# Inverses of the delta-rule blocks in a two-layer hybrid backbone: 8 by 8 diagonal blocks by forward substitution on GpSimd, the highest level in quarters of 64

## What is computed

```python
decay = _masked_exp(gam[..., :, None] - gam[..., None, :], incl)
a_strict = jnp.where(strict, jnp.einsum('bchtk,bchsk->bchts', kb, kc) * decay, 0.0)
lhs = a_strict + jnp.eye(CHUNK, dtype=a_strict.dtype)
sol = lax.linalg.triangular_solve(lhs, rhs, left_side=True, lower=True, unit_diagonal=True)
```

## Time and profile before

| what | value |
|---|---|
| runs listed | 2750.91, 2751.10, 2753.89 us, median 2751.1 |
| profiled execution: span | 2753.8 us (the slowest listed time is 2753.89) |
| TensorE busy | 2452.9 us, 89% |
| VectorE busy | 1261.2 us, 46% |
| ScalarE busy | 653.6 us, 24% |
| GpSimd busy | 609.6 us, 22% |
| scans of layer 0 | about 307 to 657 us |
| scans of layer 1 | about 1752 to 2043 us |

### The profile page before, as it was taken

The page is one execution under the profiler, slowest core; times in us unless marked ns, Lnnn a source line. Parts: engine busy times, 40 slices in busy tenths (PEclk is TensorE's granted clock), DMA queues, the critical chain, the costliest instruction groups (busy, mean ns, idle before and its releaser), DMA issues.

```text
span 2753.8 us, 45775 instructions
## 1 busy us (share of the span) xinstructions
PE 2452.9 (89%) x15116; PEld 1641.3 (60%) x15117; DVE 1261.2 (46%) x2828; ACT 653.6 (24%) x1191; POOL 609.6 (22%) x640
## 2 busy tenths in 40 slices
PE   5999888888989999999996898888888999999996
PEld 2437788887745555555554345788876555555553
DVE  4442487877433333333333453467863333333333
ACT  2116342432201111111111214523221111111111
POOL 0000244532002222222221000235320122222221
PEclk9999899999989999999998899999999999999997
DMA  7642200002539999999996352200026899999994
GB/s 264 244 168 80 32 1 1 1 1 67 229 111 349 358 357 350 337 343 340 363 339 194 133 184 61 50 1 1 1 67 263 305 370 369 387 353 367 372 367 158
DMA packets 187953, 574.27 MB, mean 209 GB/s; under 512 B 55774, under 2 KB 99110, under 8 KB 148902
## 3 DMA queue, kind: packets, MB, share of 16 engines
q1 hardware_dynamic: 162982, 520.48, 50.8%
q0 software_dynamic: 24832, 51.97, 8.0%
HBM read 554.89 MB, written 53.15 MB: 221 GB/s over the span
## 4 chain that ended last, share of the span: by engine, by line
PE 62%; DMA 13%; DVE 12%; issue 5%; ACT 4%; POOLq 2%; DVEq 2%; ACTq 1%; POOL 0%; SPq 0%
PE ps L1815 56%; DMA featT<-ffn_rows,idx_in 8%; PE ps L1819 5%; DVE R L1157 3%; DMA R<-ffn_rows,idx_in 3%; ACT R L864 2%; POOLq L776 1%; DMA R<-in_exp_up 1%; DVE R L1436 1%; DVE ring L1157 1%; DVE featT L1157 1%; DVE R L1160 1%; DVEq L1154 1%; ACT L864 1%; DVE h L1157 1%
## 5 line engine op out<-in xcount | busy, mean ns | idle before, releaser
L1815 PE MATMUL ps<-R 128*64 128x256 f32 (+6 forms) x9232 | 1433.8, 379 | 62.9 <-DVEq L1441 16.0
L1815 PEld LDWEIGHTS ps<-R 128*64 128x64 f32 (+2 forms) x9232 | 887.2, 162 | 476.2 <-issue 251.7
L864 ACT ACTIVATE R<-ps 128x256 f32<-128x256 f32 (+3 forms) x395 | 175.4, 444 | 1073.0 <-PE ps L1815 1027.4
L1157 DVE TENSOR_TENSOR R<-R,ps 128x256 f32<-128x256 f32 (+2 forms) x256 | 151.0, 590 | 445.9 <-ACT R L864 367.1
L1815 PE MATMUL ps<-featT,ring 128*128 128x512 f32 (+1 forms) x768 | 312.8, 564 | 0.3 <-issue 0.3
L1815 PEld LDWEIGHTS ps<-featT,ring 128*128 128x128 f32 x768 | 147.0, 195 | 161.4 <-issue 156.5
L1160 DVE TENSOR_SCALAR R<-ps,idx_out 128x512 f32<-128x512 f32 x128 | 96.1, 751 | 271.4 <-PE ps L1815 271.4
L1815 PE MATMUL ps<-ring,R 128*128 128x128 f32 (+2 forms) x1008 | 205.9, 331 | 15.4 <-DVE ring L1157 9.5
L1166 DVE COPY R<-ps 128x512 f32<-128x512 f32 (+2 forms) x280 | 153.8, 549 | 131.4 <-PE ps L1819 101.7
L701 POOL TENSOR_TENSOR R<-ring,lev 128x512 f32<-128x512 f32 x56 | 72.2, 1290 | 614.1 <-DVEq L1398 308.4
L800 POOL DMA_INDIRECT ffn_sum_even<-R,idx_out x64 | 94.5, 1476 | 482.1 <-DVE idx_in L1157 354.9
(11 more groups left out here) (200 smaller groups left out, 1989.3 us busy)
## 6 DMA issues: line engine op xcount, KB each, us to landing
R<-in_exp_gate SPq DMA_DIRECT2D x128, 1024.0 KB, 9.4
R<-in_exp_up SPq DMA_DIRECT2D x128, 1024.0 KB, 19.2
R<-in_exp_down SPq DMA_DIRECT2D x128, 1024.0 KB, 19.3
R<-in_w_mod SPq DMA_DIRECT2D x48, 1024.0 KB, 6.9
ring<-in_w_in SPq DMA_DIRECT2D x30, 1024.0 KB, 5.3
ring<-in_w_out SPq DMA_DIRECT2D x4, 1024.0 KB, 6.8
R<-in_w_out SPq DMA_DIRECT2D x4, 1024.0 KB, 6.4
ffn_sum_odd<-zero SPq DMA_DIRECT2D x6, 512.0 KB, 11.1
```

The source lines that it names most:

```text
L864: do(C.activation(out_, in_, func, **kw), name)
L1157: do(V.tensor_tensor(out_, a, b, op), name)
L1815: return MM(out_, lhsT, rhs, start=start, stop=stop)
```

## The change

The three lowest levels go. In their place, for each unit, the 8 by 8 blocks on the diagonal are inverted by substitution:

1. ScalarE copies the four 32x32 diagonal squares of each head out of A (`own_quarters`, four copies of 32 rows).
2. GpSimd masks and folds them to one 8-column block per row, and spreads each element against the unit vectors (`own_blocks`, four operations).
3. TensorE multiplies by a block-of-ones matrix, so that every row of an 8-block holds all elements of its block (`repeats`, one product of 256 columns); ScalarE copies that out (`repeats_copy`).
4. GpSimd does seven dependent steps of a multiplication and a subtraction of 4 to 28 elements per row, and writes the result with one 128x512 product as block diagonal into W (`own_inverse`).
5. TensorE transposes the four heads, ScalarE copies them to the other half of W.

Three levels follow as before (`MID` = 3, blocks of 16, 32, 64), with both halves of W of one layout. The highest level works on quarters: 4 products of 64x64, a copy of 64 rows, 4 products of 64x64, and a negated copy by ScalarE straight into W. The work that stood between seven levels is dealt out again over these steps; `levels_abs` and `levels_exp` now stand together at the end of a unit on ScalarE (`states`), `keys(u + 1)` stands before the third subtraction on VectorE, and VectorE has no subtraction of a highest level. Seven operations are added to VectorE's constants at the start. Waits on `sp_x`, `sp_done` and `cum_dve` become waits on one counter, `sp_dve`.

```diff
+BLK = 8
+L0 = 3
+MID = LEVELS - 1 - L0
+NP, NQ = 2 * MID + 3, 2 * MID + 1
...
+                def own_blocks(u):
+                    wait("dq_sb", u + 1, l)
+                    do(G.tensor_tensor(dq[:, :, :], dq[:, :, :], blkq[:, :].unsqueeze(1).to_broadcast([P, HH, 32]), ALU.mult))
+                    do(G.tensor_tensor(d16[:, :, :], dq[:, :, 0:16], dq[:, :, 16:32], ALU.add))
+                    do(G.tensor_tensor(dc[:, :, :], d16[:, :, 0:BLK], d16[:, :, BLK:16], ALU.add))
+                    if u:
+                        wait("pre_ps", 3 * u, l)
+                    do(G.tensor_tensor(dx[:, :, :], dc[:, :, :].rearrange("p q t -> p (q t)").unsqueeze(2).to_broadcast([P, HH * BLK, BLK]),
+                                       unit8[:, :].unsqueeze(1).to_broadcast([P, HH * BLK, BLK]), ALU.mult), "nt_ready")
+                def own_inverse(u):
+                    d = UNITS[u][1]
+                    do(G.tensor_copy(dv[:, :, :], unit8[:, :].unsqueeze(1).to_broadcast([P, HH, BLK])))
+                    wait("rep_sb", u + 1, l)
+                    rep = dr[:, :, :].rearrange("p (q t) r -> p q t r", q=HH)
+                    for n in range(BLK - 1):
+                        r, to = (n, slice(n + 1, BLK)) if d == 0 else (BLK - 1 - n, slice(0, BLK - 1 - n))
+                        do(G.tensor_tensor(dt8[:, :, to], rep[:, :, to, r], dv[:, :, r:r + 1].to_broadcast([P, HH, BLK - 1 - n]), ALU.mult))
+                        do(G.tensor_tensor(dv[:, :, to], dv[:, :, to], dt8[:, :, to], ALU.subtract))
+                    if u >= 2:
+                        wait("vn_ps", u - 1, l)
+                    do(G.tensor_tensor(W[u % 2][:, 1, :, :].rearrange("p q (b t) -> p q b t", t=BLK), dv[:, :, :].unsqueeze(2).to_broadcast([P, HH, P // BLK, BLK]),
+                                       blk[:, :].rearrange("p (b t) -> p b t", t=BLK).unsqueeze(1).to_broadcast([P, HH, P // BLK, BLK]), ALU.mult), "nt_ready")
...
+                own_blocks(0)
+                own_inverse(0)
                 masked(0, 0)
...
-                    masked(u, 2)
                     if wanted:
                         do(levels_mul(late, u, hq[:, :, tk(c)]), "hl_ready")
-                    masked(u, 3)
+                    masked(u, 2)
-                    masked(u, 4)
-                    masked(u, 5)
-                    masked(u, 6)
...
+                        own_blocks(u + 1)
+                        own_inverse(u + 1)
                         masked(u + 1, 0)
                         masked(u + 1, 1)
...
+                def own_quarters(u):
+                    wait("at_ready", 2 * u + 1, l)
+                    if u:
+                        wait("nt_ready", (u - 1) * (MID + 2) + 1, l)
+                    for b in range(4):
+                        own = slice(32 * b, 32 * b + 32)
+                        ins = C.activation(dq[own, :, :], AT[u % 2][own, :, own], ACT.Identity)
+                    do(ins, "dq_sb")
+                def repeats_copy(u):
+                    wait("pre_ps", 3 * u + 3, l)
+                    f(dr[:, :, :].rearrange("p a r -> p (a r)"), ps[:, 1, 2 * P:4 * P], ACT.Identity, "rep_sb")
...
+                def states(u):
+                    levels_abs(u)
+                    levels_exp(u)
...
-                levels_abs(0)
                 e_gdn(0)
+                own_quarters(0)
+                repeats_copy(0)
+                states(0)
...
-                    levels_exp(u)
+                    for hf in range(2):
+                        half_copy(u * NP + hf + 1, hf, W[u % 2][:, 0, :, :])
                     if un > 1:
                         wait("ho_ps", un - 1, l)
                     f(eb[:, :], bh[:, :], ACT.Exp, "eb_ready")
-                    if u + 1 < U:
-                        steps(Mg, u + 1, range(HS, NDEC))
-                    act.drain().then_inc(S["m_ready"], 1)
-                    for j in range(1, LEVELS):
...
+                    wait("p_ps", (u + 1) * NP, l)
+                    f(Pm[hi, :, 0:HD], ps[hi, 1, 0:HH * HD].rearrange("p (h t) -> p h t", h=HH), ACT.Identity, "p_sb")
+                    if u + 1 < U:
+                        own_quarters(u + 1)
+                    wait("q_ps", (u + 1) * NQ, l)
+                    f(W[u % 2][lo, 1, :, hi], ps[lo, 3, 0:HH * HD].rearrange("p (h t) -> p h t", h=HH), ACT.Identity, "p_sb", scale=-1.0)
+                    if u + 1 < U:
+                        repeats_copy(u + 1)
...
                     if u + 1 < U:
-                        levels_abs(u + 1)
+                        states(u + 1)
...
+            ts(levt[:, 1, :], levt[:, 0, :], L0, None, ALU.logical_shift_right)
+            cp(blk[:, :], levt[:, 1, :])
+            ts(blk[:, :], blk[:, :], 0.0, None, ALU.is_equal)
+            tt(blkq[:, :], blk[:, 0:32], blk[:, 32:64], ALU.add)
+            for b in range(2, 4):
+                tt(blkq[:, :], blkq[:, :], blk[:, 32 * b:32 * b + 32], ALU.add)
+            do(V.tensor_reduce(unit8[:, :], ident[:, :].rearrange("p (b r) -> p r b", r=BLK), AX.X, ALU.add))
...
-                    w_first(u)
                     if u:
                         hgrn_out(u - 1)
+                    if u:
                         hgrn_state(u - 1)
                         scores(u - 1)
-                    w_next(u, 1)
-                    if u:
-                        gdn_end(u - 1)
...
-                    w_next(u, 2)
+                    w_next(u, 0)
                     if u:
+                        gdn_end(u - 1)
                         ssd_out(u - 1)
+                    w_next(u, 1)
                     if wanted:
                         h_levels(u, 0)
-                    w_next(u, 3)
                     if u:
                         ssd_state(u - 1)
                     if more_:
                         hgrn_scans(u + 1)
+                        keys(u + 1)
+                    w_next(u, 2)
                     if wanted:
                         h_levels(u, 1)
                     if more_:
+                        queries(u + 1)
                         hgrn_levels(u + 1, (0, 1))
-                    w_next(u, 4)
-                    if more_:
-                        keys(u + 1)
-                        queries(u + 1)
                     if wanted:
                         h_levels(u, 2)
                     if more_:
                         hgrn_levels(u + 1, (2, 3))
-                    w_next(u, 5)
                     if wanted:
                         h_levels(u, 3)
                     if more_:
                         hgrn_levels(u + 1, (4, 5, 6))
-                    w_next(u, 6)
...
+                def repeats(u):
+                    wait("nt_ready", u * (MID + 2) + 1, l)
+                    mm(ps[:, 1, 2 * P:4 * P], blk[:, :], dx[:, :, :].rearrange("p a r -> p (a r)")).then_inc(S["pre_ps"], 1)
+                repeats(0)
...
+                    wait("nt_ready", u * (MID + 2) + 2, l)
+                    for hf in range(2):
+                        for q in range(2):
+                            ins = turn(ps[:, 1 + hf, tk(q)], Wu[:, 1, 2 * hf + q, :])
+                        ins.then_inc(S["p_ps"], 1)
...
+                        for hf in range(2):
+                            wait("p_sb", u * (NP + 1) + 2 * a + hf + 3, l)
+                            for q in range(2):
+                                got, tq = Pm[:, 2 * hf + q, :], Wu[:, 1, 2 * hf + q, :]
+                                mm(ps[:, (3, 0)[hf], tk(q)], tq, got)
+                                ins = mm(ps[:, (3, 0)[hf], tk(2 + q)], got, tq)
+                            ins.then_inc(S["q_ps"], 1)
...
+                    wait("t_ready", 2 * (u + 1) * MID, l)
+                    for q in range(HH):
+                        ins = mm(ps[hi, 1, q * HD:(q + 1) * HD], AT[u % 2][lo, q, hi], Wu[lo, 0, q, lo])
+                    ins.then_inc(S["p_ps"], 1)
+                    if wanted:
+                        wait("h_cp", (un - 1) * 4 + 2, l)
+                        h_products(u, 2)
+                    wait("p_sb", (u + 1) * (NP + 1) - 1, l)
+                    for q in range(HH):
+                        ins = mm(ps[lo, 3, q * HD:(q + 1) * HD], Pm[hi, q, 0:HD], Wu[hi, 1, q, hi])
+                    ins.then_inc(S["q_ps"], 1)
+                    if more_:
+                        repeats(u + 1)
+                    if wanted:
+                        wait("h_cp", (un - 1) * 4 + 3, l)
+                        h_products(u, 3)
+                        wait("m_ready", 3 + 2 * u, l)
+                        wait("at_ready", 2 * u + 4, l) if more_ else wait("ssd_sb", 2 * u, l)
+                        decays(u, Ms, HS, 6).then_inc(S["ssd_pre"], 1)
+                    if not last_step:
...
+                    h_out(u)
```

220 lines of the change are left out of this document (104 added, 116 removed).

## The result

| | runs shown | median | ratio to before (95% interval) |
|---|---|---|---|
| before | 2748.89 to 2757.23 us (5) | 2751.1 us | |
| changed | 2762.22 to 2778.12 us (5) | 2769.5 us | 1.0061 [1.0046, 1.0076] |

The account below looks back on a forecast made before the run. Outputting units were taken as bound by VectorE and TensorE taking turns, context units by the levels' latency. Startup +1.9, layer 0 -35.6 and layer 1 +5.5 gave -28.2 from 2751.1: 2723 us, range 2690 to 2765.

Parts of the forecast that it names:

- the period becomes 36: Scan units giving output: time from one unit's finished inverse to the next falls from 42 us to 36.
- the clock rival: TensorE idles longer per unit, so its clock falls; outputting intervals about 4 us longer, 2754 us in all; chance 0.14.
- the same 8: Layer 0's six full intervals: 8 us of low clock kept from before, added to 6 x 36 for 224.
- my own walk: Step-by-step timing of one outputting unit across the engines, from one inverse's end to the next: 36 us.
- Price of the small GpSimd operation: Each of fourteen dependent substitution operations on GpSimd: 0.44 us with its gap, in all 6.2 us.
- The chain rival: Slower GpSimd substitution steps lengthen every unit; the gain is gone at 0.62 us an operation; chance 0.18.
- ScalarE and not GpSimd releases the first level: Outputting units: ScalarE's copies after the levels' Abs and Exp start the first level, with 1.1 us to spare for GpSimd.
- VectorE alone sets the period, 33: Rival for outputting units: TensorE and VectorE overlap better, intervals of 33 us, total 2696 us; chance 0.18.
- Context interval 32.2: Layer 1's units without output: the uncovered chain gives 30.2 us, plus 2.0 for low clock, 32.2.
- Last interval 31.6: Last unit of a layer's scan, which prepares no next one: from 34.3 to 31.6 us, -2.7.
- Tail 18.1: From a layer's last finished inverse to the next stage: 18.1 us, +8.8 in each layer.
- First units: First scan unit of each layer: -7 us in layer 0, +3.5 in layer 1.

Follow-up runs that it names:

- the runs with fillers: The changed kernel with TensorE products nothing reads, placed where it idles; with 13 per unit at the unit's head alone: 2726.0 us, ratio 0.9896.
- with 10 fillers: The changed kernel with 5 unread TensorE products ahead of the replicating product and 5 ahead of the block transposes: 2731.0 us, ratio 0.992.
- The other order of ScalarE alone: The changed kernel with ScalarE's exponentials of the levels behind the two copies of the transposed blocks, not ahead: 2746.1 us, ratio 0.997.
- the run with three steps: The changed kernel with 3 of the 7 GpSimd substitution steps, its inverse not the right one: 2760.9 us, ratio 1.0022.
- kernels with head fillers: Changed kernels with unread TensorE products ahead of the replicating product and the block transposes; with 5 and 8: 2726.0 us, ratio 0.9896.

## Why the prediction was wrong

**The step that failed** is "the period becomes 36", with the sentence under the clock rival that "outputting units keep TensorE at work through most of the chain". From forecast to profile the span is 50.8 us longer (2776.4 against 2753.8 - 28.2). The eight outputting intervals that follow an outputting unit make 49.8 of it: six in layer 0 took 266.0 for 224 and two in layer 1 83.2 for 75.4; the other terms, each off by up to 6 us, cancel to 1.0. The mechanism was named as a rival at a chance of 0.14, and at half its size: it priced +4 an interval from one row at 0.89, but the clock fell three times per interval to a mean of 0.81, +8.3. In the sum, the term for the low clock was "the same 8" for six intervals; it measured 266.0 - 216 = 50. The rival, too, forecast no change where it was slower. The Trainium skill's rule of the clock gate was cited as speaking against the change, and it was right about the direction; the runs with fillers are what shows it.

Why it was mis-sized can be read in my own walk. It had TensorE waiting for the spread, for the copies and for VectorE's state, and counted these waits as time only. The sum did not ask what the clock does behind them. The old kernel already had such drops: 46.0 us at 0.89. The walk itself was near: with 10 fillers in it an interval at full clock takes 36.6 to 36.8, for the 36 of the forecast.

Point by point:

- **TensorE's and VectorE's work taken off**: right; VectorE went from 34.5 to 26.7 in an interval.
- **Price of the small GpSimd operation**: forecast 0.44, measured 0.38, between the bounds 0.22 and 0.63. The estimate from the Trainium skill's dispatch ("GPSIMD Engine Reference", section 3.1) was 0.31 for one operation without its gap and 6.9 for the fourteen; they measured 0.21 to 0.25 and 5.3, below it and below my 0.29 and 6.2. The blocks at T + 13.9 came out to the tenth, a later copy of the replicated blocks making up for the shorter steps. The chain rival, with its turn at 0.62, is out.
- **ScalarE and not GpSimd releases the first level**: right in the changed kernel, and late by a further 3.2 us for want of clock in the decays. The other order of ScalarE alone was worth 3.8 an interval at the low clock, and cost 0.7 at full clock.
- **VectorE alone sets the period, 33**: no interval between two outputting units fell under 36.1.
- **Context interval 32.2**: 30.7, 30.8 and 31.6. The 2.0 added for the clock was too much; without it the walk had 30.2, and two intervals at full clock gave back 0.9 each. Here the chain of GpSimd binds, which the run with three steps (-2.0 to -2.8) and these two intervals show from both sides.
- **Last interval 31.6**: 34.5 at 0.85; 30.1 to 31.3 in five of the kernels with head fillers.
- **Tail 18.1**: 19.2 in layer 0, at clock 0.81, and 17.0 in layer 1, at 0.96. **Startup +1.9**: TensorE's first instruction came at 24.60, +2.2. **First units** -7 and +3.5: -10.4 and -1.3.
- Some 6 us more behind the last scan of the profiled execution belong to no edit; the profiled execution is 8.7 above the median.

What stays open: why the drop behind T, and the one behind the wait ahead of the keys, is there in some intervals and not in others of the same kernel, and why the first unit of layer 0 took 43 to 56 us in kernels that differ little (at clock 0.88 and 0.79). No run separated these.
